# Index scores between the index query tiles, two blocks' sums on GpSimd, and the selection rounds laid out anew, in a four-layer decoder trunk

## The reference, cut to what matters

```
q, k, v, q_idx, k_idx, w_idx = split_last(h @ w_in, B_SPLITS)   # 16 heads, 4 kv heads, 8 index heads of 64
w_idx = w_idx * 8 ** -0.5
# per block of 128 queries:
sc    = einsum('bqhd,bsd->bqhs', qib, k_idx) * 64 ** -0.5
score = einsum('bqh,bqhs->bqs', wb, relu(sc))                    # sum over 8 index heads
score = where(causal, score, -inf)
_, sel = top_k(score, 128)                                       # then attention over the selected keys
```

## Time and profile before

| | us |
|---|---|
| median of 3 runs | 3086.8 |
| lowest and highest | 3086.34, 3088.23 |
| the profiled execution | 3086.14 |
| its span, first to last instruction | 3084.3 |
| mean granted TensorE clock | 0.977 |

### The profile page before, as it was taken

How to read it: one execution, slowest core, us unless ns; L and a number is a source line. 1 busy time by engine, 2 the same in 40 slices (tenths; PEclk the granted TensorE clock), 3 DMA queues, 4 the chain that set the end, 5 groups by cost and what they waited for, 6 DMA issues and landing times.

```text
span 3084.3 us, 37045 instructions
## 1 busy us (share of the span) xinstructions
PE 2907.0 (94%) x14448; PEld 2345.2 (76%) x14448; DVE 1055.6 (34%) x1936; ACT 1093.7 (35%) x1652; POOL 1371.1 (44%) x1073
## 2 busy tenths in 40 slices
PE   7999869999998999999899998999999998789999
PEld 5978658888765688887677776788888786568887
DVE  3023451122395511215465553311131233441112
ACT  4343432223355422233334333322233333342222
POOL 3355524444445344444243332444454554534443
PEclk9999989999999999999999999999999999899999
DMA  4222103222431123334111110233332221113322
GB/s 128 62 76 52 51 28 96 95 95 95 109 69 49 50 94 95 95 95 103 28 42 42 42 42 15 88 99 100 95 95 75 68 67 51 42 55 95 95 95 82
DMA packets 277886, 227.58 MB, mean 74 GB/s; under 512 B 30100, under 2 KB 271508, under 8 KB 277764
## 3 DMA queue, kind: packets, MB, share of 16 engines
q1 hardware_dynamic: 267024, 216.29, 23.6%
q10 hardware_dynamic: 10740, 9.65, 1.3%
HBM read 223.61 MB, written 2.30 MB: 73 GB/s over the span
## 4 chain that ended last, share of the span: by engine, by line
PE 83%; DVE 8%; POOL 4%; ACT 3%; issue 2%; DMA 0%; ACTq 0%; DVEq 0%; POOLq 0%
PE bank L1709 45%; PE bank L1646 23%; POOL w_lo L543 3%; PE bank L2055 1%; PE bank L2067 1%; PE bank L2064 1%; PE bank L1733 1%; ACT w_hi L676 1%; POOL arena L565 1%; PE bank L1794 1%; PE bank L1900 1%; DVE rs L1236 1%; PE bank L1826 1%; PE bank L1928 1%; PE bank L1812 1%
## 5 line engine op out<-in xcount | busy, mean ns | idle before, releaser
L543 POOL TENSOR_TENSOR w_lo<-raw,w_hi 128x512 fp32r<-128x512 f32 x808 | 1070.1, 1355 | 1356.1 <-ACT w_hi L676 1356.1
L676 ACT ACTIVATE w_hi<-raw 128x2048 fp32r<-128x2048 f32 x202 | 385.4, 1908 | 430.9 <-PE bank L1709 423.4
L1709 PE MATMUL bank<-h_hi,w_hi 128*128 128x512 f32 x1024 | 403.2, 394 | 0.0
L1709 PE MATMUL bank<-h_lo,w_hi 128*128 128x512 f32 x1024 | 400.4, 391 | 0.0
L1709 PE MATMUL bank<-h_hi,w_lo 128*128 128x512 f32 x1024 | 400.3, 391 | 0.0
L1709 PE MATMUL bank<-g_hi,w_hi 128*128 128x512 f32 x1024 | 398.3, 389 | 0.0
L1709 PE MATMUL bank<-g_lo,w_hi 128*128 128x512 f32 x1024 | 398.3, 389 | 0.0
L1709 PE MATMUL bank<-g_hi,w_lo 128*128 128x512 f32 x1024 | 398.3, 389 | 0.0
L1646 PE MATMUL bank<-h_hi,w_hi 128*128 128x512 f32 x784 | 337.7, 431 | 6.9 <-POOL w_lo L543 4.6
L1646 PE MATMUL bank<-h_lo,w_hi 128*128 128x512 f32 x784 | 315.5, 402 | 0.0
L1646 PE MATMUL bank<-h_hi,w_lo 128*128 128x512 f32 x784 | 315.0, 402 | 0.0
(11 more groups left out here) (246 smaller groups left out, 4325.4 us busy)
## 6 DMA issues: line engine op xcount, KB each, us to landing
raw<-in_mlp_w SPq DMA_DIRECT2D x128, 1024.0 KB, 5.3
raw<-in_a_w_in SPq DMA_DIRECT2D x48, 512.0 KB, 5.1
raw<-in_c_w_in SPq DMA_DIRECT2D x32, 512.0 KB, 5.3
raw<-in_a_w_in SPq DMA_DIRECT2D x12, 1024.0 KB, 5.0
raw<-in_b_w_in SPq DMA_DIRECT2D x18, 256.0 KB, 4.4
raw<-in_a_w_out SPq DMA_DIRECT2D x4, 1024.0 KB, 5.7
raw<-in_b_w_in SPq DMA_DIRECT2D x4, 1024.0 KB, 6.1
arena<-bias_scratch ACTq DMA_DIRECT2D x16, 256.0 KB, 3.4
```

The source lines that it names most:

```text
L543: ins = nc.gpsimd.tensor_tensor(w_lo[s][:, k, :], raw[s][:, k, :], w_hi[s][:, k, :].bitcast(F32), ALU.subtract)
L676: nc.scalar.activation(w_hi[s][:], raw[s][:], ACT.Copy).then_inc(w_hi_done, 1)
L1709: mm = nc.tensor.matmul(lin_bank[j][:], w[s][:, c, P * j:P * j + P], a[:, c, :], start=c + z == 0, stop=c == CT - 1 and z == 2)
```

## The change

PE makes a pair of index pieces after each of the last three index query tiles; one pair stands in k = 0, two each in k = 1, 2, 4 and 5. ACT follows the same order. For blocks 2 and 1 (p from 8) ACT applies the relu, waits for it, and multiplies in place by the index weight; POOL sums the eight pieces of a block, in two places of its order, under a new semaphore `idx_low`; ACT's reuse of the relu buffers waits for that from p = 14. DVE sums block 3 only. The rounds stand earlier: before tiles k = 2 to 9, none before the last two.

```
-        INDEX_AT = {(0, z): 2 * z for z in range(4)}
-        INDEX_AT.update({(2 + z // 2, 2 * (z % 2)): 8 + 2 * z for z in range(4)})
-        INDEX_AT.update({(6 + z // 2, 2 * (z % 2)): 16 + 2 * z for z in range(4)})
+        INDEX_AT = {(0, 1): 6}
+        INDEX_AT.update({(1 + z // 2, 2 * (z % 2)): 8 + 2 * z for z in range(4)})
+        INDEX_AT.update({(4 + z // 2, 2 * (z % 2)): 16 + 2 * z for z in range(4)})
...
 POOL, mixer_b
+                def low_sums(pieces):
+                    for p in pieces:
+                        b, hd = 3 - p // 8, p % 8
+                        n = P * (b + 1)
+                        pool.wait_ge(idx_relu, p + 1)
+                        r = brelu[p % 6][:, 0:n]
+                        if hd == 0:
+                            continue
+                        if hd > 1:
+                            pool.wait_ge(idx_low, p - 9 - (b == 1))
+                        other = brelu[(p - 1) % 6][:, 0:n] if hd == 1 else score[b]
+                        nc.gpsimd.tensor_tensor(score[b], other, r, ALU.add).then_inc(idx_low, 1)
...
                 for k in range(4):
                     split_ahead(n0 + k)
+                pool.wait_ge(iw_ready, 1)
+                low_sums(range(8, 16))
                 dst = bk + bq
                 for k in range(10):
                     if k:
                         qk_scale(1, Q + k - 1, dst[k - 1])
+                    if k == 2:
+                        low_sums(range(16, 24))
                     if k % 2:
                         split_ahead(n0 + 4 + k // 2)
...
 ACT, mixer_b
                     act.wait_ge(idx_done, p + 1)
-                    if p >= 6:
+                    if p >= 14:
+                        act.wait_ge(idx_low, max(1, p - 14 - (p == 23)))
+                    elif p >= 6:
                         act.wait_ge(idx_acc, p - 5)
-                    n = P * (3 - p // 8 + 1)
-                    nc.scalar.activation(brelu[p % 6][:, 0:n], bank[2 + p % 2][:, 0:n], ACT.Relu,
-                                         scale=HD ** -0.5).then_inc(idx_relu, 1)
+                    b, hd = 3 - p // 8, p % 8
+                    r = brelu[p % 6][:, 0:P * (b + 1)]
+                    ins = nc.scalar.activation(r, bank[2 + p % 2][:, 0:P * (b + 1)], ACT.Relu, scale=HD ** -0.5)
+                    if b < 3:
+                        ins.then_inc(idx_raw, 1)
+                        act.wait_ge(idx_raw, p - 7)
+                        ins = nc.scalar.activation(r, r, ACT.Copy, scale=bw[:, b, hd:hd + 1])
+                    ins.then_inc(idx_relu, 1)
...
                 for k in range(4):
                     copy_tile(t0 + 2 + k, by_block(bqi[k]), reversed_blocks(lin_bank[k % 2][:]))
+                    if k:
+                        index_relu(2 * k - 2)
+                        index_relu(2 * k - 1)
                     if k % 2:
                         round_ahead(n0 + 1 + k // 2)
...
 DVE, mixer_b
-                index_sums(range(8))
-                beside = {2: ((3, 0, 7),), 3: ((3, 7, 11),), 4: ((3, 11, 15),), 5: ((3, 15, 16),), 6: ((2, 0, 5),),
-                          7: ((2, 5, 10),), 8: ((2, 10, 14),), 9: ((2, 14, 16), (1, 0, 1)), 10: ((1, 1, 6),),
-                          11: ((1, 6, 11),)}
+                index_sums()
+                beside = {2: ((3, 0, 13),), 3: ((3, 13, 16),), 4: ((2, 0, 5),), 5: ((2, 5, 10),), 6: ((2, 10, 15),),
+                          7: ((2, 15, 16), (1, 0, 5)), 8: ((1, 5, 11),), 9: ((1, 11, 16),)}
                 for k in range(2, 12):
-                    for b, lo, hi in beside[k]:
-                        if (b, lo) == (1, 0):
-                            index_sums(range(20, 24))
+                    for b, lo, hi in beside.get(k, ()):
                         for r in range(lo, hi):
                             top(b, (r,))
-                    if k in (2, 5, 7):
-                        p = {2: 8, 5: 12, 7: 16}[k]
-                        index_sums(range(p, p + 4))
                     add_eps(1, Q + k - 2, k >= 4)
-                top(1, range(11, 16))
...
 PE, mixer_b
                 for k in range(4):
                     product(n0 + 1 + k // 2, t0 + 2 + k, H, CT, 0, 24, None, 0, None)
+                    if k:
+                        pe.wait_ge(copied, copy_first[i] + 2 + k)
+                        pe.wait_ge(ki_ready, 1)
+                        index_scores(2 * k - 2)
...
                 pe.wait_ge(copied, copy_first[i] + 6)
-                pe.wait_ge(ki_ready, 1)
```

More of the change, by code:

```diff
@@ L195, in trunk @@
         idx_done, idx_relu, idx_acc = sem("idx_done"), sem("idx_relu"), sem("idx_acc")
+        idx_low, idx_raw = sem("idx_low"), sem("idx_raw")
         topk_step, mask_ready, tm_done = sem("topk_step"), sem("mask_ready"), sem("tm_done")
@@ L1288, in mixer_b, with index_sums @@
                 dve.wait_ge(iw_ready, 1)
[L1290 to L1295, removed]
+                def index_sums():
+                    for hd in range(B_IDX):
+                        dve.wait_ge(idx_relu, hd + 1)
+                        w = bw[:, 3, hd:hd + 1]
                         if hd == 0:
-                            nc.vector.tensor_scalar(score[b], brelu[p % 6][:, 0:n], w, None, ALU.mult).then_inc(idx_acc, 1)
+                            nc.vector.tensor_scalar(score[3], brelu[0], w, None, ALU.mult).then_inc(idx_acc, 1)
                         else:
-                            dve.wait_ge(idx_acc, p)
-                            nc.vector.scalar_tensor_tensor(score[b], brelu[p % 6][:, 0:n], w, score[b], ALU.mult,
+                            dve.wait_ge(idx_acc, hd)
+                            nc.vector.scalar_tensor_tensor(score[3], brelu[hd % 6], w, score[3], ALU.mult,
                                                            ALU.add).then_inc(idx_acc, 1)
@@ L1306, in top @@
                     if 0 in rounds:
-                        dve.wait_ge(idx_acc, 8 * (4 - b))
+                        dve.wait_ge(idx_acc, 8) if b == 3 else dve.wait_ge(idx_low, 7 * (3 - b))
                         nc.vector.tensor_tensor(score[b][:, P * b:P * b + P], score[b][:, P * b:P * b + P], causal,
@@ L1862, in mixer_b, with index_scores @@
                 t0 = tile0[n0]
+                def index_scores(first):
+                    for p in (first, first + 1):
+                        b, hd = 3 - p // 8, p % 8
+                        if p >= 2:
+                            pe.wait_ge(idx_relu, p - 1)
+                        r = slice(HD * (hd % 2), HD * (hd % 2) + HD)
+                        nc.tensor.matmul(bank[2 + p % 2][:, 0:P * (b + 1)], bqi[hd // 2][r, P * b:P * b + P],
+                                         bki[r, 0:P * (b + 1)], start=True, stop=True).then_inc(idx_done, 1)
                 product(n0, t0, H, CT, 0, 24, hl_done, 16 * li, None)
@@ L1878, in mixer_b @@
                     for z in range(4):
[L1879 to L1885, removed]
+                        if (k, z) in INDEX_AT:
+                            index_scores(INDEX_AT[k, z])
                         if z == 2 and k >= 3:
```

## The result

The changed kernel is slower: median 3095.68 us of 8 runs (3093.84 to 3099.03) against 3086.62 us of 8 runs of the kernel before (3085.68 to 3094.25, where seven of the eight lie below 3089); ratio 1.0026, 95% interval 1.0015 to 1.0037. I had forecast 3087.6, no difference that can be told, range 3083.3 to 3091.3. The profiled execution took 3096.32 us with a span of 3094.5: 10.2 us more than before.

The account below looks back on a forecast made before the run. PE's idle time in mixer B's opening was taken as the bound. Terms -2.72 + 1.15 + 1.4 + 0.75 + 0.22 gave +0.8 us, so 3087.6 against the median, range 3083.3 to 3091.3.

Parts of the forecast that it names:

- What bounds the kernel, and what goes: Mixer B's opening: PE is busy 94% of the span, only its idle counts, and 2.72 us of that goes.
- 0.69, 1.58 and 0.45: PE idles in us before the first index pair and before two sum_qk with late add_eps, all forecast to go.
- part 1: Six block-3 index pieces between the query tiles: removes the 0.69 idle and starts DVE's rounds about 4 us earlier.
- Part 3: ACT's relu plus scaled copy (0.58 us for 384 columns) delays second pieces of pairs: 1.15 us new PE idle.
- Part 4: POOL's adds (1.00 us for 384 columns) stand behind a split and ACT waits: 1.4 us idle before a sum_qk.
- Parts 1 and 5: Block 3's earlier sums, and DVE's rounds in their new places, the latter costing 0.75 us new PE idle.
- rounds start near 841: DVE's rounds in mixer B's opening were to start near 841 us instead of 845.1.
- end at 860.7, before the square: The thirteen rounds before the first add_eps were to end at 860.7 us, ahead of ACT's square of tile 2.
- my 923: Forecast end in us of the last tile of mixer B's opening, with +0.8 us as the sum of changes.
- Near 911: Forecast time in us of DVE's last mask, instead of 929, with DVE about 15 us ahead.
- The tail moves along unchanged, and so does all behind it.: The 1.41 and 6.81 us idles after the last tile, and all later work, were to shift without further cost.
- Rival (b): Slower, about +9 us, 3096: idle at (3, 2) above about 3 us halves the clock for about 14 us; chance 0.07.

Follow-up runs that it names:

- e2: Kernel before, with only the six block-3 index pieces moved between the query tiles: 3088.15 us against 3087.65, ratio 1.0003.
- e10: Changed kernel plus 10 extra matmuls (2.3 us) after mixer B's first tile: 3099.50 us against 3088.19 for the kernel before, ratio 1.0034.
- e1: Kernel before plus 20 extra matmuls (4.5 us) that do nothing, after mixer B's first tile: 3095.92 us against 3087.65, ratio 1.0025.
- e6: Kernel before plus 5 extra matmuls (1.1 us) after mixer B's first tile: 3091.87 us against 3088.51, ratio 1.0011.
- e9: Changed kernel, with POOL scaling the last query tile before splitting the next weight chunk: 3090.51 us against 3088.19 for the kernel before, ratio 1.0011.
- e12: Changed kernel, four POOL adds before the split, ten rounds before the first add_eps, last query tile scaled before its split: 3090.03 us against 3088.19, ratio 1.0005.
- e15: Kernel before, last query tile scaled before the split, first attention unit's mask ahead of that scaling: 3090.44 us against 3087.43, ratio 1.0006.

## Why the prediction was wrong

- **What bounds the kernel, and what goes.** Right: PE's idle time was the measure, and 0.69, 1.58 and 0.45 went. That part 1 alone brings 0.7 and leaves the 1.58 and 0.45, e2 showed; I had given it a share of them.
- **Part 3.** Prices right within 0.05 us, the cost mis-sized. The stretched pairs cost 1.0 at (2, 2) instead of 0.45, and 1.1 at (4, 2) instead of 0.7, 0.95 more in all. At (2, 2) both sides of the wait came as forecast (PE at 854.73, the copy's end at 855.69, where I had 854.75 and 855.8); what I left out is that the second piece, started alone at 855.75, takes 0.84 to the next tile, as long as a whole unbroken pair (850.90 to 851.74).
- **Part 4.** Right to 0.1 us for the first add, its price and the square behind it. That the idle without DVE's rounds is 1.43, my 1.4, is luck: PE arrived 0.5 us later than I had it (the stretched pair), and add_eps took 1.23 instead of 0.68 beside POOL's adds. The two errors cancel.
- **Parts 1 and 5, "rounds start near 841", "end at 860.7, before the square".** Mis-sized: 843.8 and 863.4. I took the last sums as if POOL's split were not beside them, though by my own order it is. That makes the first idle 2.58 instead of 1.4, and the short low clock behind it adds 1.6; e10, with an idle of 2.59, was spared that. The later idle was 0.60, my 0.75. So the opening came to 0.8 + 0.95 + 1.2 - 0.15 + 1.6 = 4.4 instead of 0.8, and the last tile ended 3.8 us behind my 923, which by my own sign is wrong. ("Near 911" for DVE's last mask was a slip in the sum: 15 us before 929 is 914, and it came at 915.0.)
- **"The tail moves along unchanged, and so does all behind it."** The step that failed most: I put all that lies behind the opening at nothing, and it was 6.2 us at mixer C's end. The opening's 4.5 alone would have given 3090.7 for the profiled execution, within the range; with the 6.2 it is 3096.3. A shift of dense work is not neutral there, as e1 shows without the change. Every forecast of some microseconds for this kernel hangs on it.
- **Rival (b)** gave 3096, and the time was 3095.7, but not by its mechanism: it wanted an idle above 3 us, a limit that no row had shown, and a low stretch of 14 us at the first sum_qk. The idle was 2.58 and the stretch 3.4 long; the long one was 1000 us away. Its chance of 0.07 was too small mainly for that second place.

What stays open: why the same fall of the clock lasts 3.4 us when it comes at 9.86 or later and 13.7 when it comes at 9.76 or sooner. The runs show that it does, not what the chip weighs. Nor do the runs show what sets the place of the fall, or why the kernel before, whose executions may well differ as the traces do, keeps within 3 to 4 us in the later comparisons. The runs of e6, e9, e12 and e15 spread over 9 to 11 us. They look like mixtures of short and long stretches, which is not shown, as one run of each was traced; a few more runs would move their medians.

## What to carry to other kernels

Read a difference of a few microseconds stage by stage, by the n-th occurrence of an instruction that both kernels have, before explaining it by the edit, and take off what was there ahead of the edit: here more than half of it arose 950 us away. A kernel with stages in which PE works in short bursts should be tried with a few plain delays; if 2.3 us cost 9 and 3.4 cost 4, a small gain or loss of the median says nothing about the edit, and the trace of the edited stage is the better judge. When work of two SBUF inputs is moved on VectorE, look at what GpSimd does in that stretch, not only at what VectorE did.

## What the runs showed of the hardware

- An idle of 2.58 us was followed by a low clock of 3.4 us in the changed kernel and in e9, one of 2.59 by none in e10; 1.84, 1.58 and 1.43 by none. The same 4.68 us of idle at mixer C's last head was followed by 3.4 us at 1.2 GHz in before and by 13.7 in the changed kernel.
- VectorE's sum of 512 columns: 0.75 us alone, 1.6 beside GpSimd's subtraction; the small causal add 0.29 and 1.25; add_eps 0.68 alone, 1.44 beside GpSimd's adds of 384 columns, 2.12 beside one of 1024. MAX8 beside GpSimd's work: 0.69 as ever. The compare of 256 columns, of one input, 0.29 alone and 0.77 beside the subtraction. GpSimd pays as well: its four subtractions took 5.98 us beside VectorE's sums and 5.01 otherwise.
- GpSimd adds: 0.77, 1.05 and 1.27 us for 256, 384 and 512 columns. A scaled copy on ScalarE within SBUF: 0.51 and 0.62 for 256 and 384.
